# Two-block transformer kernel: GpSimd forms the experts' gate of the modulation during the in-projection instead of during the attention

## The reference

```python
mod = jax.nn.silu(c) @ w_ada[l] + b_ada[l]
sh1, sc1, gt1, sh2, sc2, gt2 = [m[:, None, :] for m in jnp.split(mod, 6, axis=-1)]
...
h = modulate(rmsnorm(x, g_mix[l]), sh1, sc1)
q, k, v, bg, cg, hv = jnp.split(h @ w_in[l], SPLIT_POINTS, axis=-1)
...
x = x + gt1 * (jnp.concatenate([att, conv], axis=-1) @ w_out[l])
h2 = modulate(rmsnorm(x, g_ffn[l]), sh2, sc2)
x = x + gt2 * expert_choice_ffn(h2, w_router[l], w_gate[l], w_up[l], w_down[l])
```

## Time and profile before

| | us |
|---|---|
| median of 3 runs | 2507.48 |
| lowest and highest run | 2506.7 and 2508.01 |
| span of the profiled execution | 2507.5 |
| TensorE busy in it | 2472.1 |
| VectorE busy | 1134.9 |
| ScalarE busy | 736.6 |
| GpSimd busy | 49.5 |

### The profile page before, as it was taken

The page is one execution under the profiler, slowest core; times in us unless marked ns, Lnnn a source line. Parts: engine busy times, 40 slices in busy tenths (PEclk is TensorE's granted clock), DMA queues, the critical chain, the costliest instruction groups (busy, mean ns, idle before and its releaser), DMA issues.

```text
span 2507.5 us, 29717 instructions
## 1 busy us (share of the span) xinstructions
PE 2472.1 (99%) x11265; PEld 1806.4 (72%) x11265; DVE 1134.9 (45%) x1730; ACT 736.6 (29%) x1051; POOL 49.5 (2%) x28
## 2 busy tenths in 40 slices
PE   9998999999999999999999999999999999999999
PEld 4876744444437888888888888888887667888887
DVE  6786412222227544436444334444337665544422
ACT  4245210100014333224333223233224354333321
POOL 0032000000000000000000000000000000000000
PEclk9999999999999999999999999999999999999999
DMA  7551699999992222312223322223322211222332
GB/s 308 177 176 61 262 411 420 421 421 421 421 409 106 101 100 102 104 63 102 97 95 101 110 83 92 94 98 105 104 86 72 80 43 39 96 92 100 105 104 68
DMA packets 84654, 404.29 MB, mean 161 GB/s; under 512 B 9176, under 2 KB 9560, under 8 KB 60896
## 3 DMA queue, kind: packets, MB, share of 16 engines
q1 hardware_dynamic: 84576, 403.22, 43.0%
HBM read 401.08 MB, written 2.10 MB: 161 GB/s over the span
## 4 chain that ended last, share of the span: by engine, by line
PE 92%; DVE 4%; ACT 2%; issue 1%; DVEq 0%; ACTq 0%
PE pair L1144 23%; PE pair L1146 23%; PE pair L1145 23%; PE pair L1436 9%; PE pair L1461 4%; PE pair L1372 2%; PE pair L1400 1%; PE pair L1691 1%; PE pair L1829 1%; PE pair L1487 1%; PE pair L1286 1%; DVE prob L2078 1%; PE pair L1799 1%; PE pair L1800 1%; PE pair L1401 1%
## 5 line engine op out<-in xcount | busy, mean ns | idle before, releaser
L1854 DVE TENSOR_TENSOR wL<-stage,wH 128x1024 fp32r<-128x1024 f32 (+3 forms) x301 | 388.9, 1292 | 774.4 <-ACT wH L699 774.0
L1144 PE MATMUL pair<-hH,wH 128*128 128x512 f32 x1672 | 658.0, 394 | 7.9 <-DVE hL L1899 2.6
L1146 PE MATMUL pair<-hH,wL 128*128 128x512 f32 x1672 | 651.3, 390 | 0.0
L1145 PE MATMUL pair<-hL,wH 128*128 128x512 f32 x1672 | 651.1, 389 | 0.0
L699 ACT ACTIVATE wH<-stage 128x1024 fp32r<-128x1024 f32 (+3 forms) x301 | 335.3, 1114 | 845.5 <-PE pair L1146 842.1
L1144 PEld LDWEIGHTS pair<-hH,wH 128*128 128x128 f32 x1672 | 314.3, 188 | 78.5 <-DVE hL L1899 4.3
L1145 PEld LDWEIGHTS pair<-hL,wH 128*128 128x128 f32 x1672 | 314.4, 188 | 66.9 <-issue 2.4
L1146 PEld LDWEIGHTS pair<-hH,wL 128*128 128x128 f32 x1672 | 314.2, 188 | 66.0
L1144 PE MATMUL pair<-gH,wH 128*128 128x512 f32 x704 | 273.9, 389 | 0.0
L1145 PE MATMUL pair<-gL,wH 128*128 128x512 f32 x704 | 273.9, 389 | 0.0
L1146 PE MATMUL pair<-gH,wL 128*128 128x512 f32 x704 | 273.9, 389 | 0.0
(11 more groups left out here) (365 smaller groups left out, 2158.4 us busy)
## 6 DMA issues: line engine op xcount, KB each, us to landing
ring<-in_experts SPq DMA_DIRECT2D x182, 1024.0 KB, 19.8
stage<-in_gate SPq DMA_DIRECT2D x88, 512.0 KB, 3.2
stage<-in_up SPq DMA_DIRECT2D x88, 512.0 KB, 3.2
stage<-in_down SPq DMA_DIRECT2D x64, 704.0 KB, 4.1
adaw<-in_w_ada SPq DMA_DIRECT2D x32, 512.0 KB, 5.0
stage<-in_w_in SPq DMA_DIRECT2D x18, 512.0 KB, 3.3
ring<-in_experts SPq DMA_DIRECT2D x16, 512.0 KB, 11.4
stage<-in_mla_in SPq DMA_DIRECT2D x9, 512.0 KB, 3.2
```

Source lines behind the costliest of these rows:

```text
L1144: pe.matmul(ps, lh, rh, start=first, stop=False)
L1145: pe.matmul(ps, lh, rl, start=False, stop=False)
L1146: return pe.matmul(ps, ll, rh, start=False, stop=last)
L1854: dve.tensor_tensor(low, stage[:, n % STAGE, 0:w], high, ALU.subtract).then_inc(strip_lo, 1)
```

## The change

GpSimd's eight tiles are brought forward. SP issues one `gate_tile` behind each of the strips s = 2 to 9 instead of all eight behind strip 17. The first two wait until the context's halves are done (its memory, `ctx`, now holds the two `gate_w` buffers), the later ones for GpSimd's additions, under a semaphore of their own, `gate_added`. GpSimd starts once five strips have been used (`strip_used >= V_AT + 1`). TensorE takes the row sum in a new function `gate_sum`, behind the scores of unit 1, into columns 40 to 47 of the PSUM bank that the other modulation sums use, and VectorE takes it with `mod_take(5)` behind unit 3. The old sum and the old addition of the bias are gone, and so are three waits for the end of the gate: before the ring's first load (`ada_added >= GATES`), before tile 17 of the ring (`mod_summed >= 6`), and on TensorE. `att_values(0)` now waits for `mod_ready >= 6`. Two semaphores are merged into others near the end of the first block (`final_normed` for `x_normed` and `rstd_both`), with the same instructions and waits.

```diff
-        gate_w = [place(f"gate_w{j}", [P, 1024], F32, at) for j, at in enumerate((G + 20 * KB, G + 35 * KB))]
-        gate_acc = place("gate_acc", [P, 1024], F32, TM + 7 * TILE)
+        gate_w = [place(f"gate_w{j}", [P, 1024], F32, at) for j, at in enumerate((G, G + 4 * KB))]
+        gate_acc = place("gate_acc", [P, 1024], F32, G + 20 * KB)
...
-        GATES = 24 + 2 * KD - 1
+        GATES = 2 * KD - 1
+        GATE_AT = 2
...
-                if j == 0:
-                    sp.wait_ge(strip_used, V_AT + 1)
+                if j < 2:
+                    sp.wait_ge(h_lo, LO0[NCTX] + KD)
                 else:
-                    sp.wait_ge(ada_added, max(24, 2 * j + 21))
+                    sp.wait_ge(gate_added, 2 * j - 3)
                 sp.dma_start(gate_w[j % 2][:, :], A["w_ada"][j * P:j * P + P, 5 * 1024:6 * 1024]).then_inc(gate_landed[j % 2], 16)
...
-            for j in range(KD):
-                gate_tile(j)
+                if GATE_AT <= s < GATE_AT + KD:
+                    gate_tile(s - GATE_AT)
...
-            sp.wait_ge(ada_added, GATES)
...
-            sp.wait_ge(mod_summed, 6)
             experts(17, 0, slot_of(17))
...
-            pool.wait_ge(out_taken, 18)
+            pool.wait_ge(cleared, 2)
+            pool.wait_ge(strip_used, V_AT + 1)
             for j in range(KD):
                 pool.wait_ge(gate_landed[j % 2], 16 * (j // 2 + 1))
...
                 if n == 0:
-                    pe.wait_ge(mod_ready, 5)
+                    pe.wait_ge(mod_ready, 6)
...
+            def gate_sum():
+
+                pe.wait_ge(gate_added, GATES)
+                pe.wait_ge(mod_ready, 5)
+                for m in range(KD):
+                    mm = pe.matmul(pb[7][:, 40 + m:41 + m], gate_acc[:, m * P:(m + 1) * P], ones[:, 0:1], start=True, stop=True)
+                mm.then_inc(mod_summed, 1)
+
             for u in range(len(UNITS) + LAG1 + 1):
                 if u < len(UNITS):
                     att_scores(u)
+                if u == 1:
+                    gate_sum()
...
-            pe.wait_ge(ada_added, GATES)
-            pe.wait_ge(shift_copied, 1)
-            for m in range(KD):
-                mm = pe.matmul(pb[3][:, m:m + 1], gate_acc[:, m * P:(m + 1) * P], ones[:, 0:1], start=True, stop=True)
-            mm.then_inc(mod_summed, 1)
-
...
                 if u <= len(UNITS):
                     att_soft(u)
+                if u == 3:
+                    mod_take(5)
...
-            dve.wait_ge(mod_summed, 6)
-            dve.tensor_tensor(mod[:, 40:48], pb[3][:, 0:KD], cols[:, COL["b_ada"][0] + 40:COL["b_ada"][0] + 48], ALU.add).then_inc(mod_ready, 1)
```

20 lines of the change are left out of this document (10 added, 10 removed).

## The result

| | before | after |
|---|---|---|
| median, us (executions) | 2507.71 (11) | 2513.75 (11) |
| lowest and highest, us | 2506.70 and 2512.19 | 2510.66 and 2519.67 |
| profiled execution: span; mean TensorE clock | 2507.5; 0.995 | 2508.9; 0.995 |

The ratio is 1.0021, with a 95% interval of 1.0013 to 1.0028: the change makes the kernel 0.2% slower, some 5 to 6 us, and the time lies outside my range. The two profiled spans differ by only 1.4 us, because the profiled execution after is the fastest of its eleven: its own time is 2510.66 us, 3.1 us under the median.

The account below looks back on a forecast made before the run. TensorE was taken to bound the kernel, so only its waits count. 2507.5 - 4.6 (attention) + 2.5 (row sum) + 1.8 (in-projection) + 0 (old place) = 2507.2 us, range 2502.4 to 2511.5 us.

Parts of the forecast that it names:

- What bounds the kernel: Whole kernel: TensorE is 92% of the chain, so a change pays only where TensorE waits and costs where it makes it wait.
- Part 1: Attention: without GpSimd's additions holding VectorE's scaling, TensorE gets back its own waits, -4.6 us, between 0 and -10.8.
- Part 2: Attention's start: the row sum ahead of unit 2's scores, at clock 0.50, costs +2.5 us, between +1.7 and +4.0.
- Part 3: In-projection: GpSimd's additions hold VectorE's two-input operations, one low half misses its deadline, +1.8 us, between 0 and +5.
- rival 3: In-projection: GpSimd's multiplications hold VectorE's two-input operations too, TensorE up to 19 us later, 2524 us; 6% with rival 5's late GpSimd.
- rival 4: The clock stays low at the attention's start (+1.5) and three in-projection deadlines are missed (+5 instead of +1.8): 2511.9 us; 11%.
- Part 4: The row sum's old place: without it TensorE's idle time is longer but ends the same, 0, between -1 and +1 us.
- SP's queue: In-projection: gate tiles waiting for GpSimd may delay strip and `ada` loads, but ScalarE's waits hide that, 0.

Follow-up runs that it names:

- trace without arithmetic: Kernel before with GpSimd's gate multiplications and additions replaced by memsets, transfers and waits kept: 2505.97 us, ratio 0.9987.
- the two kernels that work in the out-projection: Gate tiles loaded and summed during the out-projection, row sum at its old place: by GpSimd 2512.01 us, by VectorE 2505.63 us.
- the kernel with VectorE in the out-projection: Against the kernel before, VectorE sums the gate's eight tiles during the out-projection, GpSimd idle there, row sum at its old place: 2505.63 us, ratio 0.9982.
- without the sum: Changed kernel with the row sum's eight one-column products left out, GpSimd's work and the transfers kept: 2512.38 us.
- the kernel without arithmetic: Changed kernel with GpSimd's 8 multiplications and 7 additions replaced by memsets, transfers, waits and row sum kept: 2506.88 us, ratio to before 0.9992.
- additions alone: Changed kernel with seven of GpSimd's eight multiplications replaced by one-column clears, the additions kept: 2515.11 us, ratio to before 1.0027.
- multiplications alone: Changed kernel with GpSimd's seven additions replaced by one-column clears, the eight multiplications kept: 2508.42 us, ratio to before 0.9996.
- the first trace: Changed kernel unaltered, the profiled execution of its first measurement: 2510.66 us.
- the fourth trace: Changed kernel unaltered, profiled once more: 2513.73 us.

## Why the prediction was wrong

**What bounds the kernel: right.** What changed the time of the stages is idle time of TensorE or its clock.

**Part 1, GpSimd leaves the attention, -4.6: right for the stage.** The trace without arithmetic has -5.2 us in the attention, 3.1 of them in the block that I had put at 2.9; the medians say -3.0 of the whole. The scaling came back to 0.52 us on average.

**Part 2, the row sum, +2.5: right in direction, too large, and with the wrong condition.** I took the half clock at the attention's start for a property of the place. It is one of the execution: the changed kernel's traces have 0, 3.4 and 13.7 us of it, and attentions of 74.06, 75.69 and 79.84 us. So the sum must be priced between attentions with the same half clock. Without any, and without GpSimd beside them, they take 74.1 us with the sum and 73.4 to 73.5 without it (the two kernels that work in the out-projection): +0.6 to 0.7 us, under my lower bound of 1.7. The step failed in what the sum displaces, and in that no later idle time takes anything of it: without the sum TensorE waits at the same place for VectorE's masking anyway,

```profile
163.96 0.70 PE L1249 MATMUL pair<-kZ,qT 128*128 128x256 f32 x2 [1.37 <-DVE stat L2052]
```

here in the kernel with VectorE in the out-projection, at the scores of unit 2. The sum's 1.92 us and its wait of 0.59 stand in place of this 1.37, so the scores of unit 2 start only 1.0 us later than here, and 0.3 to 0.4 us of that come back later. At half clock, which I had reckoned with, the wait is shorter, 0.62 us. The 2.3 us between the medians with and without the sum don't contradict this, given their intervals.

**Part 3, GpSimd in the in-projection, +1.8: this step failed.** It says that one deadline is missed by 1.8 us. Measured were +6.45 us in the traces, and +8.5 by the medians between the kernel without arithmetic and the changed one. Three things in it were wrong.

First, I treated the deadlines one by one, each with its own slack, and wrote that the later strips "have 3 us and more and the delay moves their deadline too". The low half that failed did have 3.4 us, but TensorE's deadline had moved by only 1.6 us (0.68 + 0.87) when VectorE's holds had come to 10.1: its lateness adds up from strip to strip, less the idle time between them. The 8.8 us of idle time couldn't pay for that either, since 7.0 of them lie at or ahead of the low half at 92.33 us, and only 1.9 us of idle time were left between it and the strip that waited. That some 14 us of holds less 8.8 of idle time gives 5.2, near the 6.45 measured, would have been luck. With the deadline that I did work out the arithmetic held: its low half is late by 0.56 us in the changed kernel and by 1.98 with additions alone.

Second, that GpSimd's additions hold VectorE and "its multiplications do not" rested on one row: the scaling at 172.99 us begins 1.15 us after its multiplication. The multiplication holds too, up to about 1.3 us after its start, and that row lies at the edge of it. Alone the multiplications cost only 0.04%; on top of the additions they have a part in the holds (0.8 us at 107.37). Of the rule of the Trainium skill ("SBUF — State Buffer", section "SBUF: two separate sides"), that the two engines exclude each other for the whole instruction, the additions agree: the held operations end within 0.2 us of the addition's end and their own time together (L1918 at 97.22, L1990 at 105.03). The multiplications do not, since two-input operations run inside them undisturbed (L1993 at 96.67 in 0.68 us, with multiplications alone). So rival 3, at 2524 us, did not come.

Third, a missed deadline has a second price. Behind the 2.98 us of idle time the granted clock was 0.50 for 3.4 us, which cost another 1.7. I had a low clock in rival 4, but at the attention, not here.

**Part 4, the old place, 0: right within its bound.** The router's stage took 0.96 us more, as TensorE's clock fell 2 us earlier there (to 0.50 from 291.1 to 301.3 us, before from 292.9 to 299.7): the sums of squares at 291.09 us took 1.85 us in place of 1.03, and the affinities came later by as much. I had allowed 1 us.

**SP's queue, 0: right.** Without arithmetic the in-projection took 65.11 us with all the transfers in it, and in the changed kernel no high half waited for a transfer. GpSimd did end at 136 us and not near 124, but nobody waits for it before 167.

**The sum.** In the first trace the parts give -6.6 in the attention with the row sum in it, +6.45, +0.96 and +0.4 ahead of the in-projection: +1.2, and 1.4 us between the spans. The attention has -6.6 where -4.6 + 2.5 = -2.1 was forecast: GpSimd's leaving brought 0.6 us more, the sum cost 1.9 less, and this execution lacks the half clock, some 2.0 us (75.43 against 73.4), which no step of mine forecast and which is the luck of one execution. The median execution lies 3.1 us higher; the fourth trace, which is as long, has this in half clocks at other places. Rival 4, 2511.9 us (the clock low and more deadlines missed), was the nearest in mechanism and in time, and it had only 11%.

## What to carry to other kernels

Work moved to an idle engine is not free if that engine shares a port with a busy one: compare what the move takes from the busy engine (here 2.4 us per addition) with what the work would cost on it (1.28 us per tile, multiplication and addition in one). When holds are spread over many deadlines, add them up from strip to strip and compare the sum at each deadline with its slack and the idle time that lies between, not each hold with the slack of its own deadline. And allow for a stretch at the 1.2 GHz level behind an idle gap of TensorE in dense work: here it came behind the gap of 3.0 us in all four traces of the changed kernel and behind one of 1.98 us, but not behind one of 2.02 us, and it cost 1.7 us more.

## What the runs showed of the hardware

- GpSimd and VectorE hold each other in both directions. An addition of 128x1024 took 2.40 us alone and up to 3.44 us when VectorE was in the way; a VectorE multiply-add took 1.28 us alone and 3.32 us.
- A GpSimd multiplication of one SBUF tile by a column of scalars let two-input VectorE operations through from about 1.3 us after its start on (the kernel with multiplications alone), though it ran for 2.85 us or more.
- Two additions of 512 columns that stand right behind each other took 1.29 to 1.80 and 1.74 to 2.28 us: VectorE does get the port between them (a pair of multiply-adds from 116.84 us ended at 120.38, inside the second half, which ran from 119.26 to 121.54), but each half may wait for it anew.
- The same program had 0, 3.4 and 13.7 us at the 1.2 GHz level at the attention's start in different executions, at 2510.7, 2513.7 and 2519.1 us.
- In all of this kernel's traces the attention is longer with the half clock: 1.6 us for 3.4 us of it, 5.8 us for 13.7.
